# Attention products transposed in an encoder layer: values stationary on two column strips

## The reference, cut to what matters

```
s = jnp.einsum("bqhd,bkhd->bhqk", q, k) * (QK_DIM ** -0.5)      # 8 heads
s = jnp.where(mask, s, -inf);  p = softmax(s)
att = jnp.einsum("bhqk,bkhd->bqhd", p, v)                       # 64 value columns per head
merged = concat([rms_norm(att, g_out_attn), rms_norm(gm, g_out_gmlp)])
out = merged @ w_out                                            # 1024 x 1024
```

## Time and profile before

| | us |
|---|---|
| runs shown | 1141.88, 1139.6, 1140.12; median 1140.12 |
| profiled execution, its own time | 1144.35 |
| its span, first to last instruction | 1142.6 |
| PE busy | 1073.1 (94%) |
| DVE, ACT, POOL busy | 635.0, 272.1, 305.5 |
| mean granted TensorE clock | 0.961 |

### The profile page before, as it was taken

The page is one execution under the profiler, slowest core; times in us unless marked ns, Lnnn a source line. Parts: engine busy times, 40 slices in busy tenths (PEclk is TensorE's granted clock), DMA queues, the critical chain, the costliest instruction groups (busy, mean ns, idle before and its releaser), DMA issues.

```text
span 1142.6 us, 14253 instructions
## 1 busy us (share of the span) xinstructions
PE 1073.1 (94%) x4836; PEld 699.7 (61%) x4836; DVE 635.0 (56%) x1274; ACT 272.1 (24%) x606; POOL 305.5 (27%) x350
## 2 busy tenths in 40 slices
PE   3799999999998999999999999899999999999992
PEld 0234555555556456666676765777777777777771
DVE  2445555555556455676766678347656444444442
ACT  1232222222332223332323212121111111111110
POOL 1222222222221011110100000124534555544453
PEclk9799999999968999999999999599999999999997
DMA  9883333333344133422312128749989999989840
GB/s 309 312 350 118 141 141 142 141 142 122 120 122 127 27 103 138 157 92 83 139 51 88 74 95 320 298 145 347 349 303 342 349 348 352 347 337 353 335 165 17
DMA packets 78102, 229.78 MB, mean 201 GB/s; under 512 B 29836, under 2 KB 33567, under 8 KB 62295
## 3 DMA queue, kind: packets, MB, share of 16 engines
q1 hardware_dynamic: 50608, 198.86, 46.8%
q0 software_dynamic: 24048, 26.81, 7.0%
q10 hardware_dynamic: 3382, 3.32, 0.9%
HBM read 201.23 MB, written 88.25 MB: 253 GB/s over the span
## 4 chain that ended last, share of the span: by engine, by line
PE 84%; DVE 7%; DMA 4%; issue 2%; ACT 2%; POOL 1%; ACTq 1%; DVEq 0%; SPq 0%; POOLq 0%
PE bank L1007 16%; PE bank L1365 10%; PE bank L1367 10%; PE bank L961 10%; PE bank L1382 10%; PE bank L1174 9%; PE bank L1120 6%; PE bank L1145 5%; PE bank L989 2%; PE bank L1092 2%; PE bank L1018 1%; PE bank L973 1%; DMA grope<-in_g_knorm 1%; DMA W_in<-in_w_in 1%; PE bank L1196 1%
## 5 line engine op out<-in xcount | busy, mean ns | idle before, releaser
L1007 PE MATMUL bank<-W_in,hT 128*128 128x512 f32 (+3 forms) x432 | 181.3, 573 | 3.7 <-DMA W_in<-in_w_in 3.7
L810 POOL TENSOR_SCALAR st<-st 128x1 f32<-128x1 f32 (+5 forms) x76 | 17.6, 231 | 566.7 <-DVEq L1719 265.7
L1007 PEld LDWEIGHTS bank<-W_in,hT 128*128 128x128 f32 (+1 forms) x432 | 79.2, 186 | 96.2 <-issue 90.3
L1365 PE MATMUL bank<-WG,xT 128*128 128x256 f32 x528 | 122.4, 386 | 1.0 <-DVE xT L2350 1.0
L1382 PE MATMUL bank<-WD,hidT 128*128 128x512 f32 x264 | 118.9, 593 | 2.9 <-DVE hidT L2366 2.9
L1174 PE MATMUL bank<-W_out,mT 128*128 128x512 f32 (+1 forms) x256 | 120.5, 599 | 0.0
L1367 PE MATMUL bank<-WU,xT 128*128 128x256 f32 x528 | 119.3, 379 | 0.0
L1367 PEld LDWEIGHTS bank<-WU,xT 128*128 128x128 f32 x528 | 100.3, 190 | 13.6
L1365 PEld LDWEIGHTS bank<-WG,xT 128*128 128x128 f32 x528 | 99.8, 194 | 14.1 <-issue 1.4
L1145 PEld LDWEIGHTS bank<-vall,probT 128*128 128x128 f32 (+1 forms) x656 | 78.5, 188 | 20.7 <-issue 18.6
L2139 DVE COPY probT<-bank 128x512 f32<-128x512 f32 (+3 forms) x104 | 57.0, 548 | 59.2 <-PE bank L961 51.8
(11 more groups left out here) (319 smaller groups left out, 1475.7 us busy)
## 6 DMA issues: line engine op xcount, KB each, us to landing
WG<-in_w_gate_e SPq DMA_DIRECT2D x33, 1024.0 KB
WU<-in_w_up_e SPq DMA_DIRECT2D x33, 1024.0 KB
WD<-in_w_down_e SPq DMA_DIRECT2D x33, 1024.0 KB
ada_w<-in_w_ada SPq DMA_DIRECT2D x24, 1024.0 KB, 7.7
residual_scratch<-x_att SPq DMA_DIRECT2D x32, 512.0 KB, 4.4
kbuf<-k_scratch SPq DMA_DIRECT2D x12, 384.0 KB, 5.0
xbuf<-in_x_prompt SPq DMA_DIRECT2D x8, 512.0 KB, 3.9
W_in<-in_w_in SPq DMA_DIRECT2D x2, 2048.0 KB, 18.9
```

Of the source, the lines that this page charges most:

```text
L1007: ins = mm(ps[:R, 0:n], hT[:, place_of[t] % 2, k, :R], W_in[:, k, c0:c0 + n], start=(k == 0), stop=(k == KD - 1))
L1365: mm(psum[2][:, 0:DE], xT[:, k, :], WG[u][:, k, :], start=(k == 0), stop=(k == KD - 1))
```

## The change

The product is transposed. The values of a head (128 keys x 64 columns) are loaded, and the 128 columns of transposed probabilities stream. Two heads are done together, the even one on array columns and PSUM partitions 0 to 63, the odd one on 64 to 127, so that bank 7 holds head columns x queries: four pairs of 128 columns. This is already the layout that W_out needs, and the attention half of mT has no transposes. In exchange what was a scalar per partition is now one per column:

- `denominators`: DVE makes the reciprocals at h = 0 of the next tile; PE spreads them over the bank's layout at h = 1 by eight products of a broadcast column with the identity, again on two strips; DVE's `divide` copies them and multiplies bank 7 into `attnT`.
- `attention_squares`: ACT squares `attnT` behind the exponentials of head 3; PE's `square_sum` at h = 2 adds over partitions by four products with a column of ones; DVE copies the result, POOL makes the root as before (`attention_rows` there now waits on `s_asc`).
- `mT_`: at h = 3 PE waits until DVE has seen the root (`attention_root`), transposes it, broadcast, into one bank, and the four gated-MLP blocks into another; DVE multiplies `attnT` by the first and copies the second. mT now stands behind S.
- `O(s, pair)` runs ahead of PT of every even head, and waits for the copies of both heads.

```diff
     def beside(s, h):
...
+        if s and h == 1:
+            work = [("denominators", s - 1, 0)] + work
+        if s and h == 2:
+            work += [("square_sum", s - 1, 0)]
         if s and h == 3:
             work += [("mT", s - 1, 0)]
...
-    closing = [("W_out", LAST - 1, 4), ("W_out", LAST - 1, 5), ("rankA", 0, 0), ("mT", LAST, 0), ("W_out", LAST - 1, 6)]
+    closing = [("W_out", LAST - 1, 4), ("square_sum", LAST, 0), ("W_out", LAST - 1, 5), ("rankA", 0, 0), ("mT", LAST, 0), ("W_out", LAST - 1, 6)]
...
-        def O(s, h):
+        def O(s, pair):
...
-            pe.wait_ge(s_PT, u + 1)
+            pe.wait_ge(s_PT, s * H + 2 * pair + 2)
...
             for b, r in bl:
-                ins = mm(psum[7][:R, h * VD:(h + 1) * VD], probT[:r, u % 2, b, :R], vall[:r, slot0(t) + b, h * VD:(h + 1) * VD],
-                         start=(b == 0), stop=(b == len(bl) - 1))
...
+                for j in range(2):
+                    h = 2 * pair + j
+                    ins = mm(psum[7][j * VD:(j + 1) * VD, pair * P:pair * P + R], vall[:r, slot0(t) + b, h * VD:(h + 1) * VD],
+                             probT[:r, h % 2, b, :R], start=(b == 0), stop=(b == len(bl) - 1))
...
+        def denominators(s):
...
+            pe.wait_ge(s_asc, 3 * s + 1)
+            ps = b2.claim(pe, ("denominators", t))
+            for h in range(H):
+                ins = mm(ps[h % 2 * VD:(h % 2 + 1) * VD, h // 2 * P:h // 2 * P + R], st2[:R, sums(s) + h:sums(s) + h + 1].broadcast_to([R, VD]), ident[:R, :R], start=True, stop=True)
...
+        def square_sum(s):
...
+            pe.wait_ge(s_asq, s + 1)
...
+            for pair in range(H // 2):
+                ins = mm(ps[:R, 0:1], sqT[:, pair, :R], ones[:, 0:1], start=(pair == 0), stop=(pair == H // 2 - 1))
...
         def mT_(s):
...
-            pe.wait_ge(s_mrg, s + 1)
-            for half in range(2):
...
+            pe.wait_ge(s_asc, 3 * s + 3)
+            ps = b2.claim(pe, ("mT0", t))
+            b2.full(tr(ps[:, 0:R], st2[:R, 42:43].broadcast_to([R, P]), R), ("mT0", t))
...
         for s in range(len(seq)):
             for h in range(H):
+                if h % 2 == 0 and (s or h):
+                    O(s - (h == 0), (h // 2 - 1) % (H // 2))
                 PT(s, h)
...
+        def attention_squares(s):
+            R = ROWS[seq[s]]
+            act.wait_ge(s_Ofree, s + 1)
+            do(A(sqT[:, :, :R], attnT[:, :, :R], ACT.Square, scale=GW ** -0.5))
...
+        def divide(s):
...
+            last_read(V.tensor_copy(attnT[:, :, :R], ps[:].rearrange("p (k n) -> p k n", n=P)[:, :, :R]), ("denominators", t), b2)
+            dve.wait_ge(s_heads, s + 1)
+            do(V.tensor_tensor(attnT[:, :, :R], attnT[:, :, :R], psum[7][:].rearrange("p (k n) -> p k n", n=P)[:, :, :R], ALU.mult))
+            signal(s_Ofree)
...
+        def attention_root(s):
+
             rstd(signalled=True)
...
+            signal(s_asc)
```

More of the change, by code:

```diff
@@ L532, in uses @@
             return [((f"{work}{half}", t), 1) for half in range(2)]
+        if work in ("denominators", "square_sum"):
+            return [((work, t), 1)]
         if work == "fold":
@@ L546, in build_in @@
                 order2 += uses(*work)
+    order2 += uses("denominators", LAST, 0)
     for work in closing:
@@ L1152, in mT_ @@
             R = ROWS[t]
-            pe.wait_ge(s_mrg, s + 1)
-            for half in range(2):
[L1155 to L1158, removed]
+            pe.wait_ge(s_asc, 3 * s + 3)
+            ps = b2.claim(pe, ("mT0", t))
+            b2.full(tr(ps[:, 0:R], st2[:R, 42:43].broadcast_to([R, P]), R), ("mT0", t))
+            pe.wait_ge(s_ld2["gm"][s % 2], 16 * (s // 2 + 1))
+            ps = b2.claim(pe, ("mT1", t))
+            for j in range(4):
+                ins = tr(ps[:, j * P:j * P + R], merged[:R, s % 2, GW + j * P:GW + (j + 1) * P], R)
+            b2.full(ins, ("mT1", t))
         def out_(s, part):
@@ L1324, in _ @@
                 for name, of, part in beside(s, h):
-                    if name != "mT":
-                        work_of[name](of, part)
-                if (s or h) and not turning:
-                    O(s - (h == 0), (h - 1) % H)
-        O(LAST, H - 1)
+                    work_of[name](of, part)
+        denominators(LAST)
+        O(LAST, H // 2 - 1)
         for name, of, part in closing:
@@ L1617, in _ @@
                 exps(s, h)
+                if s and h == 3:
+                    attention_squares(s - 1)
                 if s >= 2 and h == 3:
@@ L2106, in mT_ @@
             R = ROWS[t]
-            for half in range(1 if s == LAST else 2):
-                tag = (f"mT{half}", t)
-                ps = b2.read(dve, tag)
-                last_read(V.tensor_copy((mT_last if s == LAST else mT)[:, 4 * half:4 * half + 4, :R], ps[:].rearrange("p (k n) -> p k n", n=P)[:, :, :R]), tag, b2)
+            dst = mT_last if s == LAST else mT
+            ps = b2.read(dve, ("mT0", t))
+            last_read(V.tensor_tensor(dst[:, 0:4, :R], attnT[:, :, :R], bcast(ps[:, 0:R].unsqueeze(1), [P, H // 2, R]), ALU.mult), ("mT0", t), b2)
+            if s < LAST:
+                ps = b2.read(dve, ("mT1", t))
+                last_read(V.tensor_copy(dst[:, 4:8, :R], ps[:].rearrange("p (k n) -> p k n", n=P)[:, :, :R]), ("mT1", t), b2)
             signal(s_mT)
@@ L2145, in PT, with denominators @@
             signal(s_PT)
-        def attention_rows(s):
+        def denominators(s):
             t = seq[s]
@@ L2191, in work @@
                 fold()
+            if name == "denominators":
+                divide(of)
+            if name == "square_sum":
+                square_sum(of)
+            if name == "mT":
+                mT_(of)
         row_max(0, 0)
@@ L2197, in _ @@
                 PT(s, h)
+                if s and h == 0:
+                    denominators(s - 1)
                 if s and h == 3:
-                    mT_(s - 1)
+                    attention_root(s - 1)
+                if s == LAST and h == 7:
+                    denominators(LAST)
                 if s * H + h + 2 < len(seq) * H:
```

79 lines of the change are left out of this document (43 added, 36 removed).

## The result

The changed kernel takes 1159.26 us (median of 4 runs, 1158.24 to 1159.69), the kernel before 1141.0 (4 runs beside it): ratio 1.0141, 95% interval 1.0117 to 1.0165. It is slower, by 18 us where 3.5 were forecast, and outside the range of 1132 to 1152. The profiled execution of the change spans 1156.5 us against 1142.6: 13.9 of the 18 us, since it is the fastest of the four and the profiled one before (1144.35) is slower than its median.

The account below looks back on a forecast made before the run. The prediction took PE's program order as the clock of the attention stage. Work of -4.1 and waits of +7.6 us gave +3.5 on the median of 1140.12, so 1143.6 us, range 1132 to 1152.

Parts of the forecast that it names:

- what PE waits for: Attention stage and closing: waits added and removed by the change, +7.6 us in sum.
- A pair's wait for the second head's probT copy: Before a product pair: the wait is covered by an S and work of 2 us or more; no cost.
- Work: PE's work: cheaper products and switches, -18.8 and -1.2, against denominators, square sum and fewer transposes, +15.9; sum -4.1 us.
- Root wait: PE before mT, each prompt tile: waits for the late root behind DVE's residual and sum copy; +10.3 us.
- The first pair behind the divide: First pair of a tile: PE waits for psum[7], freed by DVE's divide; +0.5 us in all, +1.2 in tile 1.
- PT(4) behind mT's multiply: PT(4) may find its bank held by DVE's delayed multiply, mostly at n = 5 and 6; +1.0 us.
- Waits that go: Transposes in front of which PE waited for probT's copies: those waits vanish, -2.8 us.
- The clock: Early tiles: a further half-clock stretch, given no term in the sum; only the slower rival counted it.
- rival B: DVE falls behind, PT(4) and W_out(0) wait longer, early tiles may run at lower clock; 1151.6 us, chance 0.17.
- Closing: Closing part: PE's 1.59 us wait for the merged rows goes, since DVE divides before pick_expert; -1.6 us.
- A: Before mT: the root isn't waited for, or the stall comes out of later waits; 1133.3 us, chance 0.29.
- C: Strips don't overlap for full 64-column loads: +37 us, 1181, chance 0.05; or +80, 1224, chance 0.01.

Follow-up runs that it names:

- before_paired_late: Kernel before, with only the change's places: two heads' products issued together ahead of the even head's PT, mT behind S of head 5; 1164.68 us.
- three_slots: Changed kernel with a third probT buffer replacing one of four key buffers, pairs 0 and 2 moved behind the side work of heads 2 and 6; 1141.33 us.
- root_direct: Changed kernel with square sum and h2T transposes ahead of W_out's parts, and PE's mT waiting on POOL's signal of the root instead of DVE's; 1153.6 us.
- before_paired: Kernel before, with a pair's two products issued together ahead of the even head's PT, mT staying right behind PT(3); 1183.91 us.
- resched: root_direct with mT ahead of S of head 5 on PE and ahead of the row maximum on DVE; 1165.33 us.
- sq_first: Changed kernel with the square sum ahead of W_out's part, and of the residual on DVE, at head 2; 1160.16 us.
- one_strip_b: Changed kernel with both heads' products on the same strip, one after the other, the second overwriting the first; 1190.89 us, one run.

## Why the prediction was wrong

**The step that failed** is the part on what PE waits for. The new place of the products enters it only with what a pair itself waits for, the divide and, in the sentence "A pair's wait for the second head's probT copy is covered by an S and work of 2 us or more", the copy. That sentence held: waits for probT came to 0.5 us. What the old place had covered stood at nothing, without a reason: I priced the pair's own waits and those for the new signals, and moved the products at no cost. I never asked what each product had been standing in front of. Before, a product stood between the side work of a head and the next PT; paired, every second PT follows the side work directly and claims a ring bank that DVE has just been asked to empty. before_paired_late shows what that costs by itself, together with mT's place, 22 us of stage, and three_slots shows it by its return. The two listings of PE's order ahead of the prediction show it: before, a product run stands ahead of every transpose run; in the changed one the square sum stands there. I read them for mT alone.

The forecast of +3.5 was -4.1 of work and +7.6 of waits. The profiled executions show, with the closing part, about -9.6 of work, and in the stage +16.7 of idle and +8.3 of clock. So waits and clock together are some 17 us off, and 5.5 us of work saved beyond the forecast hide part of it.

Point by point:

- **Work, -4.1.** Measured -9.9 in the stage and +0.3 in the closing part: right sign, sized too small. A pair of 28 passes takes 1.68 us to the next start and one of 32 takes 1.90 (chain of three_slots), 0.055 a pass as assumed (0.056); what remains for a group, with the slower PT behind it (0.91 for seven transposes against 0.77), is 0.28 in place of 0.34: 2.5 us over the 32 pairs. The sample tile I took to be "load-bound both ways", saving 1.2, at 0.15 for a change to or from the 64-row block, a price that I gave without a row. Two heads of it now take what one took, 20 passes in 0.87 us (359.30 to 360.17) against 10 in 0.87 (358.39 to 359.26): 3.5 saved over four pairs, 2.3 more than forecast. I had applied the overlap of loads on two strips to the prompt tiles and not here. Denominators: 1.02 us to the next start and 1.82 in place of 1.72 for the W_out parts behind them, so 1.12 against 1.28, 1.4 over the tiles. mT's transposes are the other way: 0.64 in place of 0.88, a gain of 0.24 and not of 0.33, 0.7 in all. That makes 5.5.
- **Root wait, +10.3.** The total fits, in part by luck, and in two places where I saw one. In tile 1 PE waits 0.49 (forecast 1.2), in tiles 2 to 4 1.84, 1.72 and 1.39 before mT (forecast 2.2, 1.9, 1.5). From tile 5 the same DVE chain, row maximum, residual, copy of the sum, holds PE one instruction earlier, at PT(3): its second bank is the square sum's. That is four waits of 1.2 to 1.3, 4.8 where 3.5 were forecast, and 5.4 + 4.8 = 10.2. Too little in the late tiles and too much in the early ones cancel.

```profile
609.17 0.95 PE L1185 MATMUL bank<-ones,sqT 128*128 128x1 f32 x8
609.98 0.63 PE L980 MATMUL bank<-ident,prob 128*128 128x128 f32 x4
611.79 0.55 PE L980 MATMUL bank<-ident,prob 128*128 128x128 f32 x3 [1.18 <-DVE st L2219]
```
```profile
609.37 0.69 DVE L2000 TENSOR_TENSOR tmp<-bank,bc_next 128x512 f32<-128x512 f32 x1 [0.18 <-PE bank L1214]
610.21 1.22 DVE L2004 TENSOR_TENSOR x_att<-x_att,tmp 128x1024 f32<-128x1024 f32 x1
611.57 0.16 DVE L2219 COPY st<-bank 128x1 f32<-128x1 f32 x1
```

  The square sum starts at 609.17, four transposes of PT(3) fill one bank, and the fifth waits until the one-column copy behind the residual is done. And the cause is not the root that I named: before_paired_late, whose mT waits for no such signal, has 8.2 us of waits at mT, and root_direct 11.1 for probT's banks, most of them at mT.
- **The first pair behind the divide, +0.5 and +1.2.** It went from 1.0 to 3.3, so +2.3 against 1.7, of which tile 1 alone is 2.12.
- **PT(4) behind mT's multiply, +1.0.** Right: 1.2 us in four waits, the longest in tiles 5 and 6.
- **Waits that go, -2.8.** They went: probT's waits fell from 4.7 to under 1.
- **Not in the sum at all:** h2T +4.6, and copies of vectors in the sample tile +2.3, with 0.5 more for one that had no wait before. Both are PTs that lost the product ahead of them.
- **The clock, 0 in the forecast, 3.4 in rival B.** Measured +8.3 in the profiled executions. It was largest where PE stood idle most, in before_paired (29.3 with 32.9 of idle) and resched (25.9 with 29.8), though not in proportion: sq_first had 30.8 of idle and 17.9.
- **Closing, -1.6.** The wait went: the merged transposes (700.77 to 701.37) have none before them, and the square sum got one of 0.32, for ACT. That it was won is not shown. Ahead of the first expert product PE now waits 5.10 for the DMA of xg where it waited 2.76. From the last PT to that product it is 0.94 shorter, with 1.4 more idle and 2.6 less for the half clock.
- **Rivals.** A fell: PE waits 10.2 us at mT and PT(3). C fell by one_strip_b; with it the rule of the Trainium skill, page TensorE: Matmul & The Clock Gate, section Part 3: Packing small matmuls, that loads overlap running matmuls only where row groups differ: both strips here use all rows, and a pass takes 0.060, not the 0.167 of a load and a stream one after the other. B had the right side, and its place (DVE's queue, PT, the lower clock) in part; at 1151.6 it had 11.5 of the 18 us, since it too began with the root.

The 22 us of the place against the 7 of the form say where the sum went wrong: not in what was added, but in what was moved.

## What to carry to other kernels

When an instruction on the bound engine is moved, list what stood behind it at the old place and which buffers that claims: the instruction was time for other engines, and the gap it leaves is a wait that no signal in the diff names. Where edits that remove a wait only rename it (square sum's bank and root together 10 us, root alone 13, probT's bank 11), stop removing signals and look for the queue that frees all three, here DVE's burst; give it work to hide behind. And price added work by taking it out in both situations: it was worth nothing in front of a wait, and about half of its size (4 of 8.9 us) once the waits were gone.

## What the runs showed of the hardware that I had not expected

- **Behind some short idles PE runs at half clock.** The half-clock stretch from 404.56 begins right behind the 1.84 us wait that ends at 404.47, the one from 612.77 one microsecond behind the 1.18 us wait that ends at 611.79. PE is busy for all of the 3.41 us that follow, at 0.50. Yet the waits of 1.72 before 439.78 and of 1.39 before 477.61 had none behind them, nor had those of 1.18 in tiles 5 and 6. I can't say which waits bring one; over the kernels with all pairs at the change's place the clock added 16 to 29 us, in the two complete ones with half the cover back 15 to 17, and before 11.5.
- **Two column strips with all rows in use run at half the time a pass, for loads of 64 columns and streams of 128 or 64:** 0.055 us by the slope between 28 and 32 passes, against 0.114 on one strip; with streams of 64, 20 passes on two strips in 0.87 us against 10 on one.
- **A group on strips shows in its neighbours:** in the chain of the change, whose pieces run to modelled ends, seven transposes take 0.91 us behind a pair and 0.77 behind W_out. By starts it is 0.82 against 0.77, and the square sum ahead of a pair takes 0.88 (598.76 to 599.64 in three_slots) against 0.81 ahead of transposes.
